# Three of eight strip pairs of each MLP's first wide pair by seven products, residual scaling in its down half

## What is computed

```python
D_MODEL = 2048; SEQ = 256; D_FF = 4 * D_MODEL; ALPHA = (2 * DEPTH) ** 0.25
def squared_relu_mlp(x, w1, w2):
    h = jax.nn.relu(x @ w1)
    return (h * h) @ w2
# once per layer, after the mixer's sublayer:
x = layer_norm(ALPHA * x + squared_relu_mlp(x, mlp_w1[layer], mlp_w2[layer]), ...)
```

## Time and profile before

| | us |
|---|---|
| median of 3 runs (2109.12 to 2110.14) | 2109.4 |
| the profiled execution | 2108.34 |
| its span | 2106.6 |
| TensorE busy in it | 2087.9 |
| VectorE busy | 1628.7 |
| ScalarE busy | 1098.6 |

### The profile page before, as it was taken

How to read it: one execution, slowest core, us unless ns; L and a number is a source line. 1 busy time by engine, 2 the same in 40 slices (tenths; PEclk the granted TensorE clock), 3 DMA queues, 4 the chain that set the end, 5 groups by cost and what they waited for, 6 DMA issues and landing times.

```text
span 2106.6 us, 26918 instructions
## 1 busy us (share of the span) xinstructions
PE 2087.9 (99%) x9824; PEld 1747.5 (83%) x9824; DVE 1628.7 (77%) x1647; ACT 1098.6 (52%) x1246; POOL 25.6 (1%) x38
## 2 busy tenths in 40 slices
PE   9999999999999999999999999999999999999997
PEld 8888887888888888888888888888888888888886
DVE  6766667869789798896687767577698978978866
ACT  5445656445555455454645554555354554645643
POOL 2000000000000000000000000000000000000001
PEclk9999999999999999999999999999999999999999
DMA  9554574566666666667564555454666666676664
GB/s 288 184 177 160 169 247 164 185 205 211 219 210 227 208 205 217 208 220 272 166 221 159 181 178 179 162 198 155 207 218 209 213 222 203 211 229 198 228 202 178
DMA packets 216122, 426.19 MB, mean 202 GB/s; under 512 B 14992, under 2 KB 50048, under 8 KB 215024
## 3 DMA queue, kind: packets, MB, share of 16 engines
q1 hardware_dynamic: 214208, 415.75, 59.6%
q0 software_dynamic: 1840, 9.44, 1.3%
HBM read 406.26 MB, written 2.10 MB: 194 GB/s over the span
## 4 chain that ended last, share of the span: by engine, by line
PE 96%; DVE 1%; DMA 1%; ACT 1%; POOL 0%; issue 0%; POOLq 0%; ACTq 0%
PE ps L1101 20%; PE ps L1103 20%; PE ps L1102 20%; PE ps L1013 10%; PE ps L1039 6%; PE ps L1041 6%; PE ps L1040 6%; PE ps L1017 5%; DMA raw<-in_ev_w_in 1%; PE ps L1214 0%; PE ps L1084 0%; PE ps L1255 0%; PE ps L1213 0%; PE ps L1218 0%; DVE w_lo L1513 0%
## 5 line engine op out<-in xcount | busy, mean ns | idle before, releaser
L1513 DVE TENSOR_TENSOR w_lo<-raw,w_hi 128x1024 fp32r<-128x1024 f32 x264 | 319.5, 1218 | 126.0 <-ACT w_hi L554 125.2
L1102 PE MATMUL ps<-raw_lo,yT 128*128 128x512 f32 x944 | 367.2, 389 | 0.0
L554 ACT ACTIVATE w_hi<-raw 128x1024 fp32r<-128x1024 f32 x256 | 267.5, 1056 | 169.9 <-PE ps L1041 114.0
L1013 PE MATMUL ps<-xT,w_hi 128*128 128x512 f32 x1016 | 258.7, 396 | 1.4 <-DVE xT L1558 1.0
L854 ACT ACTIVATE w_hi<-raw 128x1024 fp32r<-128x1024 f32 x168 | 173.7, 1050 | 144.7 <-DMA raw<-in_mlp_w 82.7
L1102 PE MATMUL ps<-raw_lo,xT 128*128 128x512 f32 x548 | 213.2, 389 | 0.0
L1013 PEld LDWEIGHTS ps<-xT,w_hi 128*128 128x128 f32 x1016 | 183.1, 188 | 35.6 <-issue 1.5
L1102 PEld LDWEIGHTS ps<-raw_lo,yT 128*128 128x128 f32 x944 | 177.2, 188 | 36.7
L1101 PE MATMUL ps<-w_hi,yT 128*128 128x512 f32 x508 | 198.0, 390 | 0.1
L1103 PE MATMUL ps<-w_hi,yT 128*128 128x512 f32 x508 | 197.7, 389 | 0.0
L854 ACT ACTIVATE more_hi<-raw 128x1024 fp32r<-128x1024 f32 x116 | 116.8, 1050 | 127.5 <-DMA raw<-in_mlp_w 127.5
(11 more groups left out here) (300 smaller groups left out, 4059.2 us busy)
## 6 DMA issues: line engine op xcount, KB each, us to landing
raw<-in_mlp_w SPq DMA_DIRECT2D x256, 1024.0 KB, 5.4
raw<-in_od_w_in SPq DMA_DIRECT2D x48, 1024.0 KB, 5.1
raw<-in_ev_w_in SPq DMA_DIRECT2D x36, 1024.0 KB, 5.1
raw<-in_ev_w_out SPq DMA_DIRECT2D x16, 1024.0 KB, 5.1
raw<-in_od_w_out SPq DMA_DIRECT2D x16, 1024.0 KB, 5.1
ks<-cross SPq DMA_DIRECT2D x256, 32.0 KB, 3.8
ks<-qs SPq DMA_DIRECT2D x256, 32.0 KB, 4.2
raw<-in_ev_w_in SPq DMA_DIRECT2D x8, 512.0 KB, 8.3
```

Source lines behind the costliest of these rows:

```text
L554: nc.scalar.activation(flat(w_hi[:, k % NSPL]), flat(raw[:, k % NRAW]), ACT.Copy).then_inc(s_hi, 1)
L1013: return nc.tensor.matmul(ps[:, f], w_hi[:, k % NSPL, i, f * P:f * P + P], both, start=k == 0 and i == 0, stop=k == BLK - 1 and i == CK - 1)
L1102: nc.tensor.matmul(out, act[0], lo, start=False, stop=False)
L1513: nc.vector.tensor_tensor(flat(w_lo[:, k % NSPL]), flat(raw[:, k % NRAW]), flat(w_hi[:, k % NSPL]).bitcast(F32), ALU.subtract).then_inc(s_ ...
```

## The change

In the first wide pair of each MLP three of the eight units become summed ones, `FIRST_UNITS = "OOSOOSSO"`, units 2, 5 and 6, on the x strips whose sums the first batch already holds (`KT_FIRST`). The constants that belong to a plan (cells, priors, summed units, strip order) are passed as a tuple `plan`, `FIRST` or `LATER`, and the counts of semaphores are shifted; the work of `pair_step` stays as it was. The written-out loops of the first pair become `first_pair` in each engine. On VectorE the second batch of `sums_of_x` moves to the place after chunk 2, `gain_residual` stays in the strip half for group 0 alone (between two weight sums of unit 2) and moves for groups 1 to 3 into the down half, `squared` moves up to the place after chunk 8, and joins and completions are added as in `pair_step`. The second batch of sums lies in `sm` and no longer in `late`, which the weight sums need. ScalarE copies the first product's bank before it waits for the end of the strip half. The core of the diff (renamed arguments and unchanged bodies are left out):

```diff
+FIRST_UNITS = "OOSOOSSO"
+KT_FIRST = (0, 1, 4, 2, 3, 5, 6, 7)
...
+        width = 2 if k < DOWN and k // 2 in FIRST_SUMMED else 1
+        cell[k] = at % (2 * NSPL) if k < JOIN else RING_CELL[k]
...
+FIRST = (FIRST_CELL, FIRST_PRIOR, FIRST_SUMMED, KT_FIRST)
+LATER = (RING_CELL, RING_PRIOR, SUMMED, KT_PAIR)
...
-        late_sums = late[:, N_LATER * CK * S:N_LATER * CK * S + 4 * N_LATER * P]
+        late_sums = sm[:].rearrange("p a n -> p (a n)")[:, 0:4 * N_LATER * P]
...
+                    hi(0)
+                    act.wait_ge(s_sums, 8 * layer + 4)
+                    act.wait_ge(s_used, b0 * BLK + 4)
+                    nc.scalar.activation(sums_hl[0], rg_sums, ACT.Copy).then_inc(s_sum_hi, 1)
+                    hi(1)
+                    hi(2)
+                    hi(3)
+                    plain_hi(blk, 2, FIRST)
+                    summed_hi(blk, 2, done, FIRST)
+                    for k in range(6, 10):
+                        hi(k)
+                    plain_hi(blk, 5, FIRST)
+                    hidden_hi(0, 1, (b0 + 1) * BLK)
+                    summed_hi(blk, 5, done, FIRST)
+                    plain_hi(blk, 6, FIRST)
+                    summed_hi(blk, 6, done, FIRST)
+                    hi(14)
+                    hi(15)
+                    hi(DOWN)
+                    copy_first_product(blk, 2 * FIRST_SUMMED[-1] + 2)
+                    act.wait_ge(s_sums, 8 * layer + 8)
+                    act.wait_ge(s_used, blk * BLK + DOWN)
+                    nc.scalar.activation(cells_hl[0][:, 0:4 * N_LATER], late_sums.rearrange("p (n s) -> p n s", s=P),
+                                         ACT.Copy).then_inc(s_sum_hi, 1)
+                    for k in range(DOWN + 1, PAIR_CHUNKS):
+                        hi(k)
...
+                    for u, kind in enumerate(FIRST_UNITS):
+                        if kind == "S":
+                            starts, last = (4, 5, 6, 7) if u == FIRST_SUMMED[0] else (), u == FIRST_SUMMED[-1]
+                            if u == FIRST_SUMMED[0]:
+                                pe.wait_ge(s_block_tr, h0 + 2)
+                                pe.wait_ge(s_sum_lo, 2 * layer + 1)
+                            plain_products(blk, u, done, starts, last, FIRST)
+                            summed_products(blk, u, starts, last, FIRST)
+                        else:
+                            for n in range(CK):
+                                wide_chunk(blk, 2 * u + n, FIRST_CELL[2 * u + n], CK * KT_FIRST[u] + n,
+                                           (0, 1, 2, 3) if u + n == 0 else (), u + n == BLK)
+                    down_pair(blk + 2, layer * (PAIRED - 1), FIRST_CELL, h0 + 2, n0)
...
+                    lo(0)
+                    dve.wait_ge(s_sum_hi, 2 * layer + 1)
+                    nc.vector.tensor_tensor(sums_hl[1], rg_sums, sums_hl[0].bitcast(F32), ALU.subtract).then_inc(s_sum_lo, 1)
+                    lo(1)
+                    blocks_turned((b0 + 2) * BLK, 4, 1)
+                    lo(2)
+                    for part in range(5):
+                        sums_of_x(part, 1)
+                    lo(3)
+                    dve.wait_ge(s_sums, 8 * layer + 8)
+                    sums(2, 0)
+                    gain_residual(n, 0)
+                    sums(2, 1)
+                    sums(2, 2)
+                    plain_lo(blk, 2, done, FIRST)
+                    summed_lo(blk, 2, FIRST)
+                    for k in range(6, 9):
+                        lo(k)
+                    squared(0, 1)
+                    lo(9)
+                    sums(5, 0)
+                    hidden_lo(0, 1)
+                    sums(5, 1)
+                    sums(5, 2)
+                    plain_lo(blk, 5, done, FIRST)
+                    sums(6, 0)
+                    summed_lo(blk, 5, FIRST)
+                    sums(6, 1)
+                    sums(6, 2)
+                    plain_lo(blk, 6, done, FIRST)
+                    summed_lo(blk, 6, FIRST)
+                    for k in range(14, DOWN + 1):
+                        lo(k)
+                    dve.wait_ge(s_hlo, h0 + 2)
+                    join_products(turn, 1)
+                    lo(DOWN + 1)
+                    join_products(turn, 2)
+                    join_products(turn, 3)
+                    join_products(turn, 4)
+                    lo(DOWN + 2)
+                    lo(DOWN + 3)
+                    dve.wait_ge(s_used, blk * BLK + DOWN)
+                    dve.wait_ge(s_prod, turn * 4 + 4)
+                    complete(2, prod_2_4)
+                    lo(DOWN + 4)
+                    complete(0, prod_1_3)
+                    dve.wait_ge(s_final, turn * 2 + 1)
+                    blocks_turned(blk * BLK + DOWN, 2, 0)
+                    lo(DOWN + 5)
+                    dve.wait_ge(s_final, turn * 2 + 2)
+                    blocks_turned(blk * BLK + DOWN, 0, 1)
+                    lo(DOWN + 6)
+                    first_add(0)
+                    gain_residual(n, 1)
+                    lo(DOWN + 7)
+                    gain_residual(n, 2)
+                    lo(DOWN + 8)
+                    gain_residual(n, 3)
+                    lo(DOWN + 9)
+                    dve.wait_ge(s_sum_hi, 2 * layer + 2)
+                    cells = [v[:, 0:4 * N_LATER] for v in cells_hl]
+                    nc.vector.tensor_tensor(cells[1], late_sums.rearrange("p (n s) -> p n s", s=P), cells[0].bitcast(F32),
+                                            ALU.subtract).then_inc(s_sum_lo, 1)
+                    lo(DOWN + 10)
+                    lo(DOWN + 11)
+                    first_add(1)
+                    lo(DOWN + 12)
+                    lo(DOWN + 13)
+                    squared(2, 0)
+                    lo(DOWN + 14)
+                    lo(DOWN + 15)
+                    dve.wait_ge(s_gained, n * GROUPS + GROUPS)
```

More of the change, by code:

```diff
@@ new lines, in pair_step @@
+                def pair_step(i):
+                    blk = i * PAIR_BLOCKS + (b0 + 2 + PAIR_BLOCKS)
+                    done = summed_before(layer, i)
+                    pe.wait_ge(s_block_tr, i * 2 + (h0 + 4))
+                    for u, kind in enumerate(UNITS):
+                        if kind == "S":
+                            first, last = u == SUMMED[0], u == SUMMED[-1]
+                            starts = (0, 1, 2, 4, 5, 6, 7) if first else ()
+                            if first:
+                                pe.wait_ge(s_sum_lo, 2 * layer + 2)
+                                pe.wait_ge(s_added, i * 4 + (n0 + 3))
+                            plain_products(blk, u, done, starts, last, LATER)
+                            if first:
+                                pe.wait_ge(s_added, i * 4 + (n0 + 4))
+                            summed_products(blk, u, starts, last, LATER)
+                        else:
+                            for n in range(CK):
+                                wide_chunk(blk, 2 * u + n, RING_CELL[2 * u + n], CK * KT_PAIR[u] + n,
+                                           (3,) if u == UNITS.index("O") and n == 0 else (), u + n == BLK)
+                    down_pair(blk + 2, i + (layer * (PAIRED - 1) + 1), RING_CELL, i * 2 + (h0 + 4), i * 4 + (n0 + 4))
@@ L1406, in mlp @@
+                first_pair()
                 with pe.Fori(0, PAIRED - 3) as i:
@@ L2047, in weight_sums @@
                     else:
-                        dve.wait_ge(s_wsum, turn * (3 * NS) + (3 * e + part))
+                        dve.wait_ge(s_wsum, done * 3 + (3 * e + part))
                         out, a, b = ((t[T_2], w_22, t[T_1]), (t[T_4], w_21, t[T_2]))[part - 1]
@@ L2135, in complete, with first_pair, lo, sums @@
                     nc.vector.tensor_tensor(ps[:, bank:bank + 2], ps[:, bank:bank + 2], joined, ALU.add).then_inc(s_final, 1)
+                def first_pair():
+                    blk, done, turn = b0 + 2, layer * (NS_FIRST + (PAIRED - 2) * NS), layer * (PAIRED - 1)
+                    def lo(k):
+                        chunk_lo(blk, k, FIRST_CELL[k])
+                    def sums(u, part):
+                        weight_sums(blk, u, done, part, FIRST)
+                    def first_add(nb):
+                        dve.wait_ge(s_gained, n * GROUPS + nb + 1)
+                        add_down(blk, 0, nb, DOWN + 4 * nb + 4)
+                    lo(0)
[70 more added lines that the diff above has]
+                    dve.wait_ge(s_gained, n * GROUPS + GROUPS)
@@ L2146, in sums @@
                     def sums(u, part):
-                        weight_sums(blk, u, turn, part)
+                        weight_sums(blk, u, done, part, LATER)
                     sums(0, 0)
```

251 lines of the change are left out of this document (96 added, 155 removed).

## The result

| | before | changed |
|---|---|---|
| median, us | 2109.26 (2108.14 to 2110.14, 12 runs) | 2113.97 (2112.86 to 2115.61, 12 runs) |
| profiled execution, us | 2108.34 | 2115.61 |
| its span | 2106.6 | 2113.8 |

The account below looks back on a forecast made before the run. TensorE was taken as the bound (busy 2087.9 of 2106.6 us, 96% of the chain). Saving and waits summed to +2.3 us in the first MLP and +3.7 in the second, +6.0 on 2109.4: 2115.4 us, range 2111.5 to 2119.5.

Parts of the forecast that it names:

- The saving: First wide pair of each MLP: nine matmuls fewer, 18 in all at 0.2267 us each, saving 4.1 us.
- Unit 2: Strip half: TensorE waits 1.79 us for the plain blocks' low part and 0.46 for the summed blocks', in each MLP.
- The down half: Chunks 18, 23, 24 and 25 come late from VectorE by 0.34, 0.19, 0.80 and 0.80 us in each MLP.
- The second MLP's extra 1.3 us: Second MLP's strip half: moves arrive 1.3 us later at `squared`, giving waits of 0.5, 0.4 and 0.5 us.
- The signs: First pair: TensorE waits for named low parts; strip halves 43.7 us (first MLP) and 45 (second), down half 46.2.
- the late moves: Second MLP's strip half: the second lot of moves there 1.3 us later, so `squared` and units 5 and 6 wait.
- The fallen clock: Rival: a pause drops TensorE to 1.2 GHz for one unit in each MLP, +17 us, 2126; chance 0.02.
- The lead that holds: Rival: VectorE has its low parts ready in both halves, saving whole, -4.1 us, 2105.3; chance 0.07, wholly or nearly.
- That the lag stays in the pair: End of the first pair: VectorE some 5 us later, next pair's weight sums done by 475.5, before TensorE's end at 481.4.

Follow-up runs that it names:

- The reordered kernel with the last scaling one place earlier: The reordered kernel with the scaling of group 3 moved ahead of chunk 26's low part: 2103.64 us, ratio 0.9974 to the kernel before.
- the first experiment: Changed kernel with one ScalarE instruction moved, chunk 17's high part ahead of the wait for the strip half's end: 2108.63 us, ratio 0.9998 to the kernel before.
- the second: Kernel before with only the scalings of column groups 1 to 3 moved into the down half, all units ordinary: 2108.80 us, ratio 0.9999.
- the third: Changed kernel with the scalings of groups 1 to 3 left in the strip half, behind chunks 6, 7 and 8: 2123.83 us, ratio 1.0074 to the kernel before.
- the three reordered ones: Changed kernel's instructions in another order, 2105.62 us; that with chunk 17's high part behind ScalarE's wait again, 2106.70; the first with group 3's scaling one place earlier, 2103.64.
- the reordered kernel: Changed kernel, scalings 0 and 1 behind the first join, 2 and 3 behind chunks 23 and 26, chunk 17's high part early, `squared` and `hidden_lo` later: 2105.62 us.

## Why the prediction was right, point by point

**The saving** was counted right: 18 matmuls fewer, at the same distance (0.2267 between starts on either side of the waits). The reordered kernel with the last scaling one place earlier had nearly all of it, by its strip halves. By the Trainium skill's figure ("TensorE: Matmul & The Clock Gate", section "Wait — 56ns, not 53.3ns?") the saving would be an estimated 0.2 us smaller; the traces have 0.2267 between starts, and the times can't tell the two apart.

**Unit 2** was put at 1.79 and 0.46. Measured in the second MLP: 2.04 and 0.39. Over the two profiles of the changed kernel the idle part was 1.85, 1.80, 1.80 and 1.30 us, and with chunk 17's high part ahead, which leaves this stretch as it was, 1.32 and 1.46. It follows where VectorE stands at the start of the pair: its turn (`blocks_turned`) began 0.7 us behind the pair's first matmul where the idle part was 1.80 or 1.85, and 0.2 to 0.4 behind it where it was 1.30 to 1.46.

**The down half** was put at 0.34, 0.19, 0.80 and 0.80 for chunks 18, 23, 24 and 25. Measured: 0.31, 0.09, 0.84 and 0.74, in the second MLP. That they come from the lead is shown by the first experiment. That chunks 23 to 25 need joins, completions and scalings together is shown by the second (scalings alone) and the third (joins and completions alone), and the strip half's lack of room by the third.

**The second MLP's extra 1.3 us** was the step that failed, and it makes up the difference between 6.0 and 4.7. It rested on the second lot of moves being issued in 5.91 us there and landing later. In the changed kernel the same eight took 5.06:

```profile
1478.63 0.59 SPq L428 DMA_DIRECT2D raw<-in_mlp_w  x1
1479.26 5.06 SPq L422 DMA_DIRECT2D ks<-qs  x8
```

VectorE was at `squared` at 1485.96 without a wait, and units 5 and 6 had none. The last move of the lot in the second MLP, before and then changed (issue in ns, start; issue to landing in us):

```profile
L411 SPq DMA_DIRECT2D ks<-qs x1: 1443/1443/1443, 1478.8 to 1478.8; - x1
DMA to landing us min/median/max: 3.0/3.0/3.0
...
L422 SPq DMA_DIRECT2D ks<-qs x1: 596/596/596, 1483.7 to 1483.7; - x1
DMA to landing us min/median/max: 1.9/1.9/1.9
```

Two things went wrong. The size: before, the last move was issued 4.47 us after the first in the second MLP as in the first. The 0.85 was its own longer issue and no later start, so it should not have been added to the landing, and the lot was there 1.0 us later and not 1.3. And the term was carried over to a kernel in which it doesn't arise. It is no accident of one execution: in the second MLP the last move landed 2.4 to 3.2 us after its issue in all seven traces in which TensorE has no wait at unit 2 (before, scalings alone, chunk 17 ahead in the kernel before, the three reordered ones, scaling 0 behind the join), and 1.9 to 2.2 in all five in which it has one. The forecast put that wait into the same pair and left the landing as it was. Why the landing follows it was not tested. The mechanism behind the term exists: with VectorE 2.4 us earlier at `squared`, the moves did set the end (2.91 us idle), and the second MLP, where the last one landed 3.2 us after its issue, lost 0.7 us more. Without this term the sum is 2 x 2.34 = +4.7.

**The signs** that the prediction named came out for the down halves (46.2, measured 46.17 twice) and crosswise for the strip halves: 43.7 and 45 were expected, 45.2 and 44.0 measured. In the profiled execution the two pairs took 6.3 us more than before, near the 6.0 forecast by luck, since a fallen clock in the first MLP (1.2 us) took the place of the late moves in the second. The other profile of the changed kernel, with neither, has 4.8, and the median 4.7.

**The fallen clock** was a rival at 0.02, which was too low. It came in one MLP of the profiled execution and cost about 1.2 us there (1.5 of slow matmuls, less the 0.4 that unit 2's summed products then didn't wait). The argument that no wait was over 2 us was no argument: 1.85 was followed by a fall in one case, while 1.80, 1.80, 1.30 and, with the scalings in the strip half, 2.45 were not. How often it comes in the runs that make the median is not known; the two with the lowest mean clock, 0.997, were the two slowest of twelve. The Trainium skill's warning ("TensorE: Matmul & The Clock Gate", section "HAM oscillation — how this bites in real kernels") of pauses that rethrottle the array is borne out in kind, by the falls behind waits of 1.85, 2.15 and 3.38 us.

**The lead that holds** would have been -4.1 and was excluded by the queue as counted. The reordered kernels show what it takes: not less work on VectorE, but two scalings (4.8 us) where it was idle, the other two farther apart, chunk 17's high part early, and `squared` not ahead of unit 5's sums.

**That the lag stays in the pair** held for the changed kernel: its list has no wait in the later pairs. It was close to failing. The addition of the last column group in the next pair started 0.4 us after the pair's end there, which TensorE didn't feel, and 1.1 us after it in the reordered kernel, where it cost 0.55.

## What to carry to other kernels

Where the bound engine is fed by another through an in-order queue, compare the lead at each hand-over, not the busy shares: a change that saves matmuls and adds vector work pays only if the new work stands in time that is idle now, and the instruction that makes that time idle (here a high part queued behind an unrelated wait) can be worth more than the change. After removing a wait, look for what the freed engine reaches next, such as a transfer, before counting the gain. And when a term rests on how long a transfer took, look at the one transfer that counts, its start and its landing, and ask whether the change moves the work that stood around it: the late moves that this forecast counted on were there in every trace without a wait at unit 2 and in none with one.

## What was not expected of the hardware

A wait of TensorE of 1.85 us was once followed by 3.4 us at a granted clock of 0.50, with matmuls of 512 columns 0.43 us apart in place of 0.2267, and so was one of 2.15 us; waits of 1.30 to 1.80 us and of 2.43 and 2.45 us were not, and waits of 3.38 us were, both times. Length alone doesn't decide it. Each idle time of TensorE at a granted clock of 1.00, from 0.03 to 2.45 us, cost another 0.08 to 0.11 us in the distance of the next matmul.
